# A weight block's split cut into smaller pieces and placed later, the attention's last transposes two turns on, and GpSimd's table loads behind the fourth modulation block

## The reference, cut to what matters

```
def adaln(cond, w, b):                      # block 1: six rows of 1024 per layer
    m = jax.nn.silu(cond) @ w + b
...
# block 1, layer 0: h = modulate(x, ...), GQA || bidirectional mLSTM, then a 16-expert MoE
# block 1, layer 1: pooling mixer, then a 16-expert MoE
...
def diff_rwkv_mixer(h, w_in, w_out, ...):   # block 2, layer 0
    z = h @ w_in
    ...
    oa = diff_attention(qa, ka, va, lam)
    oa = rms_norm(oa, subln) * (1.0 - lam_init)
    ob, v_b = rwkv7_time_mix(zb, mu, vec, w_up, a_up, g_up, v_first, vres)
    mix = jnp.concatenate([oa.reshape(Bn, S_, A_WIDTH), ob.astype(h.dtype)], axis=-1)
    return mix @ w_out, v_b
```

## Time and profile before

| what | us |
|---|---|
| median of 3 runs | 2535.5 |
| lowest, highest | 2534.52, 2540.42 |
| the profiled execution | 2537.42 |
| its span in the trace | 2535.6 |
| the four modulation blocks in (start of the fourth product) | 38.38 |
| first product of block 2's first mixer to its last | about 1504 to 1742 |

### The profile page before, as it was taken

One profiled execution on the slowest core, in us unless ns is written; L12 is line 12 of the kernel. 1 busy time (PEld: TensorE's weight loads), 2 busy tenths in 40 slices (PEclk: granted clock), 3 DMA queues, 4 the chain that ended last, 5 costly groups with the idle time before them and its releaser, 6 DMA issues.

```text
span 2535.6 us, 36106 instructions
## 1 busy us (share of the span) xinstructions
PE 2107.0 (83%) x16306; PEld 1511.3 (60%) x16306; DVE 911.8 (36%) x1314; ACT 740.9 (29%) x1126; POOL 104.4 (4%) x140
## 2 busy tenths in 40 slices
PE   4998976666667776666669999979999999999999
PEld 2764542222223532222229988968998998978997
DVE  3655440000002310000016446666445444445633
ACT  3333310000001200000015446346445444354542
POOL 2100000000000000000000101000100100000110
PEclk8999988888889898888879999989999999999999
DMA  8369779999999399999995544206555555534542
GB/s 282 108 220 387 276 334 423 427 428 427 428 427 413 154 428 428 428 426 428 427 394 174 164 168 159 76 36 202 172 186 192 179 183 195 196 133 156 185 165 101
DMA packets 200025, 679.28 MB, mean 268 GB/s; under 512 B 7952, under 2 KB 101296, under 8 KB 175552
## 3 DMA queue, kind: packets, MB, share of 16 engines
q1 hardware_dynamic: 195328, 664.49, 67.6%
q0 software_dynamic: 2496, 7.24, 0.8%
q10 hardware_dynamic: 2048, 5.24, 0.6%
HBM read 675.90 MB, written 1.05 MB: 267 GB/s over the span
## 4 chain that ended last, share of the span: by engine, by line
PE 56%; DMA 34%; DVE 5%; ACT 3%; SPq 1%; issue 1%; DVEq 0%; ACTq 0%
PE ps L253 45%; DMA ring<-in_w_exp_gate 11%; DMA ring<-in_w_exp_down 10%; DMA ring<-in_w_exp_up 9%; DMA ring<-in_w_mod 4%; PE ps L1858 2%; PE ps L2614 2%; DVE ring_r L679 2%; PE ps L1873 1%; PE ps L782 1%; ACT ring_r L670 1%; PE ps L611 1%; DMA ring<-in_ffn_wgu 1%; PE ps L620 1%; PE ps L621 1%
## 5 line engine op out<-in xcount | busy, mean ns | idle before, releaser
L253 PE MATMUL ps<-HH,ring_r 128*128 128x256 f32 x2720 | 536.9, 282 | 2.7 <-DVE ret_V L3434 2.2
L253 PEld LDWEIGHTS ps<-HH,ring_r 128*128 128x128 f32 x2720 | 435.1, 189 | 6.5 <-DVE ret_V L3434 2.7
L1858 PE MATMUL ps<-ring,XS 128*32 128x256 f32 x4096 | 293.6, 438 | 155.7 <-DMA ring<-in_w_exp_gate 108.9
L679 DVE TENSOR_TENSOR ring_r<-ring,ring_r 128x2048 fp32r<-128x2048 f32 (+2 forms) x152 | 325.4, 2180 | 193.5 <-ACT ring_r L670 193.4
L1858 PEld LDWEIGHTS ps<-ring,XS 128*32 128x32 f32 x4096 | 137.5, 123 | 339.2 <-DMA ring<-in_w_exp_gate 162.7
L253 PE MATMUL ps<-HL,ring_r 128*128 128x256 f32 x1136 | 318.7, 281 | 0.0
L670 ACT ACTIVATE ring_r<-ring 128x2048 fp32r<-128x2048 f32 (+2 forms) x152 | 269.2, 1821 | 126.6 <-PE ps L253 73.7
L1873 PE MATMUL ps<-ring,AT 128*32 128x512 f32 x960 | 160.7, 805 | 139.2 <-DMA ring<-in_w_exp_down 136.5
L2082 ACT ACTIVATE SG<-ps 128x256 f32<-128x256 f32 x32 | 12.3, 384 | 819.5 <-PE ps L1858 808.6
L253 PEld LDWEIGHTS ps<-HL,ring_r 128*128 128x128 f32 x1136 | 214.1, 188 | 0.4 <-issue 0.2
L1973 DVE TENSOR_TENSOR AA<-SG,ps 128x256 f32<-128x256 f32 x32 | 13.5, 421 | 516.7 <-PE ps L1858 516.7
(11 more groups left out here) (557 smaller groups left out, 2842.2 us busy)
## 6 DMA issues: line engine op xcount, KB each, us to landing
ring<-in_w_exp_gate SPq DMA_DIRECT2D x64, 2048.0 KB, 36.0
ring<-in_w_exp_up SPq DMA_DIRECT2D x64, 2048.0 KB, 36.1
ring<-in_w_exp_down SPq DMA_DIRECT2D x64, 2048.0 KB, 36.6
ring<-in_ffn_wgu SPq DMA_DIRECT2D x88, 1024.0 KB, 7.7
ring<-in_w_mod SPq DMA_DIRECT2D x24, 2048.0 KB, 13.7
ring<-in_ffn_wd SPq DMA_DIRECT2D x20, 2048.0 KB, 7.8
ring<-in_odd_w_in SPq DMA_DIRECT2D x12, 2048.0 KB, 7.9
ring<-in_even_w_in SPq DMA_DIRECT2D x6, 2048.0 KB, 8.5
```

The costliest lines, as they stand in the source:

```text
L253: ins = e.matmul(out, l, r, start=start and i == 0, stop=stop and i == n - 1, skip_group_check=True)
L679: v.tensor_tensor(lo[:, c], s[:, c], hi[:, c].bitcast(F32), ALU.subtract).then_inc(*E.up("split_dve", name, q))
L1858: ins = e.matmul(self.GU[which][32 * j:32 * j + 32, :], self.XS[:, 4 * hk + k, 32 * n:32 * n + 32], W[:, k, 256 * j:256 * j + 256], start= ...
```

## The change

Four edits in `Rwkv` and one in `Kernel.gpsimd`.

1. `("out0", 1)` leaves `SPLIT_AT` (it stood at turns 25 and 26). ScalarE now splits its two halves at turns 25 and 27, at the end of the turn and no longer at its beginning; VectorE subtracts four quarters of 128x1024 at turns 26, 28, 30 and 32, at the end of the turn.
2. The eight transposes of `dif_OA` stand two turns later on TensorE, and so does everything behind them in `pe_dif`.
3. Their low parts on VectorE and their high parts on ScalarE stand two turns later.
4. GpSimd waits for the fourth modulation block before its first load, and issues the tables and routers (L1708, L1710) ahead of the loads of single floats (L748, L750).

```
-                (20, 21, ("out0", 0)), (25, 26, ("out0", 1)))
+                (20, 21, ("out0", 0)))
...
-        for turn in range(27):
+        for turn in range(22):
...
+    def act_last_split(self, a, w):
+        for q in range(2):
+            self.S.parts.act(a, w, ("out0", 1), (q,))
+            yield
+            yield
+
+    def dve_last_split(self, v, w):
+        E, name = self.S.E, ("out0", 1)
+        s, hi, lo = self.S.parts.views(name)
+        for q in range(4):
+            c = slice(q * D, (q + 1) * D)
+            w.wait_ge(E.at("split_act", name, q // 2))
+            v.tensor_tensor(lo[:, c], s[:, c], hi[:, c].bitcast(F32), ALU.subtract).then_inc(
+                *(E.up("split_dve", name, q // 2) if q % 2 else E.up("split_dve")))
+            yield
+            yield
...
-        yield
-        yield
+        for _ in range(4):
+            yield
         S.pe_columns(e, w, "dif_pe", ("oa",), halves(self.OA), 4, two, ("dif_dve", "dif_dve"), E.at("dif_dve", "oa"))
...
+                after_steps(26, self.dve_last_split(v, w)))
...
-        yield
-        yield
+        for _ in range(4):
+            yield
         S.dve_column_parts(v, w, "dif_dve", ("oa",), *self.MA, "dif_pe", "dif_act", lambda k: self.sub)
...
+                after_steps(25, self.act_last_split(a, w)))
...
         a.activation(s8, s8, ACT.Sqrt, scale=1.0 / 128, bias=S.eps).then_inc(*E.up("dif_act", "root"))
-        yield
+        for _ in range(3):
+            yield
...
         S, E, w = self.S, self.S.E, Waits(g)
+        w.wait_ge(E.at("loaded", ("mod", 0, 3)))
+        self.even.pool_loads(g)
         self.start.pool(g, w)
-        self.even.pool_loads(g)
         self.even.pool(g, w)
```

More of the change, by code:

```diff
@@ L2803, in dve @@
         S.parts.dve_next(v, w, ("mix0", 1024))
-        in_turn(self.splits(S.parts.dve, v, w), self.dve_pieces(v, w), after_steps(self.CHAIN, self.dve_rwkv(v, w)), after_steps(self.ATTENTION, self.dve_dif(v, w)))
+        in_turn(self.splits(S.parts.dve, v, w), self.dve_pieces(v, w), after_steps(self.CHAIN, self.dve_rwkv(v, w)), after_steps(self.ATTENTION, self.dve_dif(v, w)),
+                after_steps(26, self.dve_last_split(v, w)))
         S.parts.dve_next(v, w, ("out0", 0), ("out0", 1))
@@ L3080, in act @@
             a.activation(self.VA[:, t, :], B.of("dif", "v", t), ACT.Copy).then_inc(*E.up("dif_act", "v", t))
-        in_turn(self.splits(S.parts.act, a, w), self.act_pieces(a, w), after_steps(self.CHAIN, self.act_rwkv(a, w)), after_steps(self.ATTENTION, self.act_dif(a, w)))
+        in_turn(self.splits(S.parts.act, a, w), self.act_pieces(a, w), after_steps(self.CHAIN, self.act_rwkv(a, w)), after_steps(self.ATTENTION, self.act_dif(a, w)),
+                after_steps(25, self.act_last_split(a, w)))
         S.parts.act_next(a, w, ("out0", 0), ("out0", 1))
```

## The result

| kernel | median us | runs | lowest, highest |
|---|---|---|---|
| before | 2535.01 | 6 | 2530.67, 2540.42 |
| changed | 2526.19 | 6 | 2523.66, 2528.17 |

The ratio is 0.9966, with a 95% interval of 0.9953 to 0.9978: 8.8 us between the medians, where 8.6 had been forecast. The profiled execution of the changed kernel took 2523.66 us (span 2521.9), 2.5 under its median; that of before lay 1.9 over the one that the prediction went by. Of all executions on record one, of the kernel before beside four of the experiments, took 4018.33 us, and it counts in no ratio.

What follows compares the result with a forecast made beforehand. Bound by the modulation weights' DMA at the start, then a chain nearly throughout on TensorE late in the mixer. Loads 4.3, split 3.6 and transposes 0.7 sum to 8.6 us, from 2535.5 to 2526.9; range 2521 to 2532.

Steps and rivals of the forecast that it cites:

- loads: At the start: GpSimd's loads leave the modulation weights' stretch, fourth product earlier; gain 4.3 us, range 3.3 to 5.0.
- split: In the mixer: copy of the inverse no longer waits behind the first split; gain 3.7 + 0.8 - 0.9 = 3.6 us.
- transposes: At the mixer's last chunk: chunk starts before the transposes, low parts' wait goes; gain 0.7 us, range -0.9 to 1.5.
- the lost rate: At the start: 360 and 309 instead of 387 GB/s beside GpSimd's loads, 1.4 us, added for the upper end 5.0.
- 0.9 us for the quarters: In the mixer: four quarters cost 4.6 us less 3.9 hidden in VectorE's exponential waits, 0.7, with some waste 0.9.
- the upper end, 5.7: Split in the mixer: one attention unit fewer at half clock gives 2.1 us more than 3.6.
- Now the chunk starts at 1710.2, 0.75 us earlier: Mixer's last chunk: starts once its state is ready, ahead of the transposes; 14.15 us on to the 72 products, gain 0.7.
- The port: Start: GpSimd's issues beside `ev_HL` slow VectorE, 4.5 us and the loads' gain lost, 2531.4; chance 0.12 with late tables.
- The late tables: Start: tables delaying `w_in_even`'s first large block past 47.3 would lose time; forecast hidden, 3.7 us spare; 0.12 with port.
- The quarters: Mixer rival: quarters not hidden, ScalarE's halves delaying the exponential or a copy; -0.9 for 3.6, 2531.4; chance 0.12.
- The clock did not stay full: Mixer rival judged here: TensorE's clock stays full after 1668, 2.1 us better, 2524.8; chance 0.08.
- The slower case: Start rival: the 96 products left at 1.2 GHz double their 22.76 us, 2549.7; chance 0.03.

Runs made afterwards that it cites:

- loads_only: Before with only GpSimd's loads put behind the fourth modulation block, tables and routers first; 2530.18 us, ratio 0.9984.
- mixer_only: The changed kernel with GpSimd's loads put back, so before with the three mixer edits; 2530.40 us, ratio 0.9989.
- norm_old_loads: norm_behind with GpSimd's loads issued at once, as before; 2525.14 us, ratio 0.9958 to before.
- norm_behind: The changed kernel with VectorE's norm two turns later, behind the last new state and the copy UB; 2521.32 us, ratio 0.9946 to before.
- split_only: Before with only the last split in its new place and in quarters, transposes and loads unmoved; 2531.08 us, ratio 0.9990.
- transposes_only: Before with only the transposes and their low and high parts two turns later; 2535.31 us, ratio 1.0012.
- norm_and_transposes: transposes_only with VectorE's norm also moved behind the last new state, split and loads as before; 2529.21 us, ratio 0.9979 to before.
- floats_wait: Before with tables and routers issued first and at once, only the single floats waiting for the fourth modulation block; 2534.57 us, ratio 0.9998.

## Why the prediction was right, and where it was not

The edits' worth from the timed ratios, each times 2534 us, over pairs that differ in that edit alone:

| edit | pairs | mean | forecast |
|---|---|---|---|
| loads | before and loads_only 4.1; mixer_only and changed 5.8; norm_old_loads and norm_behind 3.0 | 4.3 | 4.3 |
| split | before and split_only 2.5; transposes_only and mixer_only 5.8; norm_and_transposes and norm_old_loads 5.3 | 4.5 | 3.6 |
| transposes | before and transposes_only -3.0; split_only and mixer_only 0.3 | -1.4 | 0.7 |

Each pair is uncertain by 2.5 to 5 us, so their means by 2 to 2.5. The sum, 7.4, agrees with the 8.6 measured directly.

The total was right in part by luck. The split was worth as much as forecast or somewhat more, the transposes, forecast as a gain, lost by trace, and the start moved by much more in the trace than the time shows. These errors have opposite signs, and the intervals are too wide to say which term carries what.

**The loads.** The forecast's time is right, and its account of the trace is not: the fourth product came 6.1 us earlier, outside 3.3 to 5.0. The step that failed is the lost rate. I took 387 GB/s for the full rate, but without GpSimd's queue the stretch from 5 to 10 us ran at 415; and I charged the single floats nothing but their bytes, where they cost 2.0 us once the tables are away. With the product at full clock the scale of the first normalization starts 8.0 us earlier (35.63 against 43.62). Of that the timed pairs return about 4. This stays open. In the traces the shift is kept: the long product of 1116 matrices that starts at 1362.70 before starts in the seven traces with the old loads (floats_wait's among them) at 1358.4 on average and in the four with the new ones at 1351.0, 7.4 us earlier. Before's own trace is the latest of the seven by 4.3 us; without it the shift is 6.6. The profiled executions of ten of the twelve kernels lie under the medians, floats_wait's by 6.4 us. So a trace's time is not the timed run's, and what part of the shift the timed runs do not have, no run shows.

**The split.** The mechanism is as predicted up to the first two units: the copy at once, the wait for `dif_P` at 1.44 where about 1.4 was named, the next `dif_S` at 0.97 us behind the transposes instead of 1.97, the waits for the exponential gone. Measured from the inverse's product the last state comes 3.6 us earlier (44.96 to 41.36), the forecast number, but not by the forecast terms. The first transposes of `dif_P` come 3.75 us earlier (forecast 3.7) and the next two units are 1.3 us shorter. Against that the third is 0.2 us longer, and the fourth 1.3, before and after:

```profile
1691.26:1698.74 7.48, 7.48 (x92) 5.90 (x93) 3.80 (x10) 1.86 (x6) 0.00 (x0) 0.77 0.01 2
```

```profile
1675.19:1683.94 8.75, 8.75 (x93) 6.95 (x93) 4.93 (x11) 1.86 (x6) 0.00 (x0) 0.61 0.01 2
```

TensorE is busy throughout in both, at a granted clock of 0.77 and of 0.61. All six kernels with the split have 8.7 to 8.9 us here; of those without it four have 7.5 and two 6.0. The prediction's 0.9 us for the quarters looked only at VectorE's waits and had no term for this.

Nor is 44.96 firm. It isn't the only place where it stands without the split: of the four others with split and norm as before two have 45.23 and 44.91, two 42.35 and 42.61. In floats_wait, one of the two, the granted clock rises within the second unit (6.3 us at 0.62, against 7.37 at 0.50 in the earlier trace rows). In those traces the split would be worth 1.1. The 2.1 us that the upper end, 5.7, counted as the split's own can come without it. With the split the value was 41.36 or 41.37 in all three kernels that have it in quarters and the norm unmoved.

**The transposes.** The sign was wrong by the traces; of the two timed pairs one shows a loss of 3.0 us and the other no difference. The step that failed: "Now the chunk starts at 1710.2, 0.75 us earlier", with 14.0 to 14.7 us from there to the 72 products. The chunk did start 0.15 us after the state, and the wait of 0.9 for the low parts did go. But the stretch took 15.9 (1695.52 to 1708.62 + 2.79 = 1711.41). Its products had been priced at before's clock, which fell to half for 3.4 us there; in the changed kernel it did so for 6.8. (At full clock the eight transposes take 1.09 us, in norm_behind, and not the 0.8 that I had as the low end.) Before, the transposes were what TensorE did while the state was still being made; with them gone it stood 4.55 us with nothing to do, against 3.67 before. The rest is 33.2 to 33.6 us in the four kernels with transposes moved and the norm ahead, 32.1 to 32.9 in the five others, which gives a loss of 0.9 between the means. About 0.8 us of a rest goes with whether the half clock lasts 3.4 or 6.8 us, and the long one comes without the move too, in two of the five. At the same 6.8 us the move costs 0.3 to 0.4. That the longer standing brought the long half clock is therefore not shown; that a short one avoids it is: behind the waits of 1.7 us in the three kernels with the norm moved the clock stays full. The ends that I gave, -0.9 to 1.5, hold the mean loss, for a reason that I had not seen. Asking what VectorE does ahead of the state would have found the better order.

**The rivals.** The port is refuted: `ev_HL` took 4.63 us with seven issues or more beside it. By the Trainium skill (SBUF — State Buffer, Who interferes with whom) a VectorE instruction with two SBUF inputs contends with a GpSimd instruction that reads SBUF, not with one that only writes it; the trace agrees as far as an issue reads no tile, 4.63 in both kernels. The late tables did not happen, the split of `w_in_even` began at 43.28 without a wait. The quarters did not undo the gain: the first two units shrank, and what the fourth lost is told above. The clock did not stay full: the first two units had 0.59 and 0.57. The slower case, 96 products at half clock, did not come: from 42 to 50 us the granted clock was 0.66, and from 50 to 60 it was 1.00, and the ring's next subtraction on the chain, at 85.29 before, came at 77.01.

## What to carry to other kernels

When work is moved away from a place where its engine waits, ask what ends that wait on the other engine, and whether the moved work's own preparation stands ahead of it: here it did, the transposes' move alone gained nothing (by trace it lost 0.3 us or more), and the norm's move beside it brought 5.1 to 8.4 us by three timed pairs and 2.2 to 4.6 in their traces. Loads that nobody needs for 60 us belong behind the transfer that the first products wait for, the loads of single numbers too, whose bytes don't account for their cost. Of edits worth 2 to 4 us in 2535, a trace gives the mechanism and repeated timed pairs give the size; single pairs for the same edit differed here by a factor of two, and for the transposes by 3.3 us.

## What the runs showed that was not expected

Single floats in a queue of their own, 576 packets and 0.03 MB until the fourth block's product, 1.5% of the DMA engines' time, put off the four modulation blocks by 2.0 us (34.08 against 32.1), with the tables behind these blocks. The Trainium skill (DMA: Bandwidth & Descriptors, Rules for kernel authors) says that a DMA whose last dimension isn't contiguous becomes one descriptor for each element. The trace counts packets, and there are fewer of them (576, of some 50 bytes) than floats (2048), so it does not show that. That SP's queue lost 0.69 MB beside them in 10 us only the runs here tell.

The later transfer went with more than its own time lost, through TensorE's clock in the product behind it. Where that product had waited 2.6 to 2.7 us for its block its sixteen matrices took 3.64, 3.64, 2.97, 3.64 and 3.19 us. Where it had waited 0.8 to 1.5 us they took 1.92 in six kernels of seven (2.61 in mixer_only), and the five with the tables behind the fourth block are all among the six. The other two of the seven, mixer_only and split_only, had waited less only because their third product had itself run slowly, in 3.56 and 3.42 us. So in the seven kernels with the tables ahead the fourth product took 1.2 us longer on average.
